# The last four expert turns: GpSimd drains, the last expert's second up product ahead of a down product, and its rows scaled by two engines

## The reference, cut to what matters

```
x = x + einsum(mix, w_out)
xf = rms_norm(x, g_ffn)
for each expert e, for the tokens that chose it:
    y = (silu(xf @ w1[e]) * (xf @ w3[e])) @ w2[e]      # 1024 -> 512 -> 1024
    x[token] += gate * y
```

## Time and profile before

| What | us |
|---|---|
| median of three runs | 1347.95 |
| the profiled execution | 1346.08 |
| its span, first to last instruction | 1344.3 |
| busy: PE, DVE, ACT, POOL | 1231.8, 418.8, 335.1, 279.5 |
| mean granted TensorE clock, share of full speed | 0.976 |

### The profile page before, as it was taken

How to read it: one execution, slowest core, us unless ns; L and a number is a source line. 1 busy time by engine, 2 the same in 40 slices (tenths; PEclk the granted TensorE clock), 3 DMA queues, 4 the chain that set the end, 5 groups by cost and what they waited for, 6 DMA issues and landing times.

```text
span 1344.3 us, 31662 instructions
## 1 busy us (share of the span) xinstructions
PE 1231.8 (92%) x13258; PEld 870.7 (65%) x13258; DVE 418.8 (31%) x906; ACT 335.1 (25%) x782; POOL 279.5 (21%) x401
## 2 busy tenths in 40 slices
PE   4999999998899999999999889987799899999983
PEld 2554444446556666666666588654689798888871
DVE  2431411116644555544543741111011111111110
ACT  3431020025435545535544100111000000000000
POOL 1320000103222312212111012322132223333211
PEclk9999999999999999999999889998999999999998
DMA  8611120133102201201033989999999999999993
GB/s 327 248 58 39 65 70 33 46 118 113 68 23 70 80 17 65 80 17 58 29 106 142 378 304 364 363 353 385 382 375 381 379 368 376 379 377 381 378 409 88
DMA packets 44844, 278.64 MB, mean 207 GB/s; under 512 B 10232, under 2 KB 15352, under 8 KB 31948
## 3 DMA queue, kind: packets, MB, share of 16 engines
q1 hardware_dynamic: 36656, 254.80, 49.3%
q0 software_dynamic: 6800, 17.84, 5.7%
q10 hardware_dynamic: 1296, 4.72, 1.0%
HBM read 250.49 MB, written 29.83 MB: 209 GB/s over the span
## 4 chain that ended last, share of the span: by engine, by line
PE 73%; DMA 12%; issue 6%; DVE 2%; ACT 2%; POOL 2%; SPq 1%; another core or an unknown queue 1%; ACTq 0%; POOLq 0%; DVEq 0%
PE psum L1093 17%; PE psum L1157 13%; DMA arena<-in_w 11%; PE psum L996 8%; PE psum L1214 7%; PE psum L1039 5%; PE psum L1071 3%; PE psum L1165 3%; PE psum L1051 2%; PE psum L869 2%; PE psum L940 2%; PE psum L1202 2%; PE psum L884 2%; PE psum L1148 1%; PE psum L1224 1%
## 5 line engine op out<-in xcount | busy, mean ns | idle before, releaser
L1157 PE MATMUL psum<-arena 128*64 128x80 f32 (+1 forms) x5632 | 229.9, 240 | 22.7 <-issue 13.2
L1093 PE MATMUL psum<-arena 128*128 128x512 f32 (+1 forms) x576 | 241.2, 577 | 1.4 <-DMA arena<-in_w_in 1.4
L1157 PEld LDWEIGHTS psum<-arena 128*64 128x64 f32 x5632 | 217.3, 138 | 34.8 <-issue 24.2
L1093 PEld LDWEIGHTS psum<-arena 128*128 128x128 f32 x576 | 109.1, 192 | 125.1 <-issue 124.6
L996 PE MATMUL psum<-arena 128*128 128x512 f32 x288 | 126.9, 593 | 1.8 <-DVE arena L2065 1.0
L1214 PE MATMUL psum<-arena 128*64 128x96 f32 (+1 forms) x2816 | 118.8, 244 | 9.5 <-issue 7.9
L1214 PEld LDWEIGHTS psum<-arena 128*64 128x64 f32 x2816 | 114.0, 139 | 13.4 <-issue 11.5
L1735 POOL DMA_INDIRECT out_y<-arena,index_now x54 | 75.3, 1395 | 194.4 <-ACT arena L1559 129.3
L1616 POOL TENSOR_SCALAR small<-small 128x2 f32<-128x2 f32 (+4 forms) x44 | 10.4, 236 | 453.3 <-DVE small L1813 163.6
L996 PEld LDWEIGHTS psum<-arena 128*128 128x128 f32 x288 | 53.3, 190 | 63.2 <-issue 61.5
L1559 ACT ACTIVATE arena<-psum,slot_gate 96x1024 f32<-96x1024 f32 x22 | 24.4, 1111 | 270.9 <-PE psum L1224 270.9
(11 more groups left out here) (251 smaller groups left out, 1367.1 us busy)
## 6 DMA issues: line engine op xcount, KB each, us to landing
arena<-in_w SPq DMA_DIRECT2D x96, 2048.0 KB, 24.0
z_rows<-arena SPq DMA_DIRECT2D x27, 256.0 KB, 2.0
arena<-z_rows SPq DMA_DIRECT2D x9, 768.0 KB, 5.6
arena<-in_w_in SPq DMA_DIRECT2D x3, 2048.0 KB, 21.6
arena<-in_x_rows ACTq DMA_DIRECT2D x9, 512.0 KB, 4.4
arena<-in_xT_rows SPq DMA_DIRECT2D x9, 512.0 KB, 13.3
arena<-in_x_rows SPq DMA_DIRECT2D x9, 512.0 KB, 6.3
out_y<-arena SPq DMA_DIRECT2D x9, 512.0 KB, 2.6
```

Of the source, the lines that this page charges most:

```text
L1093: ins = pe.matmul(o[:, 0:w], xT[n][:, k, :], w_in[:, at_ + k * w:at_ + (k + 1) * w], start=(k == 0), stop=(k == KD - 1))
L1157: ins = pe.matmul(o[c:c + CT, j * EB:j * EB + rows], w[:, k, j * P + c:j * P + c + CT], x[:, k, 0:rows], start=(k == 0), stop=(k == KD - 1))
```

## The change

It has three parts.

1. GpSimd. `turn(p)` begins with `pool.drain()` in its last four turns, 28 to 31.
2. The order at the last expert. SP issues the w3 of turn 31 ahead of the w2 of turn 30. PE does `hidden_3(31)` ahead of `down_by_tokens(30)`. The down product of turn 31 goes to PSUM bank 5 in place of bank 4, and doesn't wait for the reading of bank 4 any more.
3. The scaling of turn 31. ScalarE scales the lower 512 columns and VectorE the upper 512, from bank 5. VectorE raises a new semaphore `y_half`, and the last scatter waits for it beside `y_read`.

```diff
@@ SP
-                def between():
+                def down_before():
                     if p > FIRST:
                         load_down(sp_, p - 1, SETS[p - 1], before_it(p - 1) + 1)
-                load_ups(sp_, p, SETS[p], before_it(p) + 1, between)
+                load_ups(sp_, p, SETS[p], before_it(p) + 1, down_before if p < NE - 1 else lambda: None)
+                if p == NE - 1:
+                    down_before()
@@ PE, expert(p)
+                    if p == NE - 1:
+                        hidden_3(SETS[p], s, b, w3_in[SETS[p]], loads_of(p), rows)
                     downs_read(b - 2, p - 2)
                     down_by_tokens(SETS[q], q, w2_in[SETS[q]], loads_of(q))
...
-                hidden_3(SETS[p], s, b, w3_in[SETS[p]], loads_of(p) + more, rows)
+                if p < NE - 1:
+                    hidden_3(SETS[p], s, b, w3_in[SETS[p]], loads_of(p) + more, rows)
@@ PE, after turn 31
             hidden_back(last)
-            downs_read(last - 1, last - 1)
-            down_by_tokens(SETS[last], last, w2_in[SETS[last]], loads_of(last))
+            down_by_tokens(SETS[last], last, w2_in[SETS[last]], loads_of(last), 5)
@@ ACT, y_take_by_tokens, half=True in turn 31
+                if half:
+                    act.activation(ye[s][0:ET, 0:BANK], bank(5)[0:ET], ACT.Copy, scale=gate_col(col)[0:ET]).then_inc(y_read, 1)
+                    return
@@ POOL, scatter, finish=True in turn 31
                 pool.wait_ge(y_read, b + 1)
+                if finish:
+                    pool.wait_ge(y_half, 1)
                 pool.wait_ge(before, count)
@@ POOL, turn(p)
+                if p + 4 >= NE:
+                    pool.drain()
@@ DVE, after hT_take(31)
+            last = dve.value_load(order_e[0:1, NE - 1:NE], min_val=0, max_val=NE - 1)
+            dve.wait_ge(yT_full, NE)
+            dve.wait_ge(ye_out[1], stores_of(NE - 3))
+            TS(ye[1][0:ET, BANK:], bank(5)[CT:CT + ET], gate_hi[CT:CT + ET, bass.ds(last, 1)], None,
+               ALU.mult).then_inc(y_half, 1)
```

More of the change, by code:

```diff
@@ L537, in build @@
         hi_ok = sem("upper_slots_ready")
+        y_half = sem("last_y_upper_half")
         tab_ok, gather_idx, scatter_idx = sem("slot_tables_ready"), sem("gather_indices"), sem("scatter_indices")
@@ L1193, in hidden_back, with down_by_tokens @@
                 ins.then_inc(ht_full, 1)
-            def down_by_tokens(w, b, arrived, count):
+            def down_by_tokens(w, b, arrived, count, to=4):
                 pe.wait_ge(arrived, count)
@@ L1201, in down_by_tokens @@
                     for i, c in enumerate((0, CT)):
-                        ins = pe.matmul(bank(4)[c:c + CT], hT[:, at_:at_ + ET], w2s[w][:, k, i * BANK:(i + 1) * BANK],
+                        ins = pe.matmul(bank(to)[c:c + CT], hT[:, at_:at_ + ET], w2s[w][:, k, i * BANK:(i + 1) * BANK],
                                         start=(k == 0), stop=(k == KF - 1))
@@ L1559, in y_take, with y_take_by_tokens @@
                 act.activation(ye[s][0:EB], bank(6, 2)[0:EB], ACT.Copy, scale=gate_col(col)[0:EB]).then_inc(y_read, 1)
-            def y_take_by_tokens(s, b, col, out_sem, count):
+            def y_take_by_tokens(s, b, col, out_sem, count, half=False):
                 act.wait_ge(yT_full, b + 1)
                 act.wait_ge(out_sem, count)
+                if half:
+                    act.activation(ye[s][0:ET, 0:BANK], bank(5)[0:ET], ACT.Copy, scale=gate_col(col)[0:ET]).then_inc(y_read, 1)
+                    return
                 act.activation(ye[s][0:ET, 0:BANK], bank(4)[0:ET], ACT.Copy, scale=gate_col(col)[0:ET])
@@ L1578, in turn @@
                 if by_tokens(p):
-                    y_take_by_tokens(p % 2, b, e, ye_out[p % 2], count)
+                    y_take_by_tokens(p % 2, b, e, ye_out[p % 2], count, p == NE - 1)
                 else:
@@ L1736, in store, with scatter @@
                                         bounds_check=last_token, compute_op=ALU.add, oob_is_err=False).then_inc(signal, 16)
-            def scatter(s, b, e, signal, before, count, rows, parts):
+            def scatter(s, b, e, signal, before, count, rows, parts, finish=False):
                 if before is signal:
@@ L1764, in turn @@
                 before = (stores_of(p - 1) if p else 0) + more
-                scatter(s, b, e, ye_out[s], ye_out[1 - s], before, CAPS[p], out_parts(p))
+                scatter(s, b, e, ye_out[s], ye_out[1 - s], before, CAPS[p], out_parts(p), p == NE - 1)
             for s in range(2):
```

## The result

The changed kernel takes 1338.96 us (median of five runs, 1337.65 to 1344.6), the kernel before 1347.95 beside it. The ratio is 0.994, 95% interval [0.9915, 0.9965]. It was timed twice more, each time beside new runs of before: 0.9943 [0.9923, 0.9963] and 0.9947 [0.9931, 0.9964]. The mean of the three is 0.9943: it gains 0.57%, some 7.6 us. The forecast was 7.35 us. The intervals are wide beside that: the first allows 4.7 to 11.5 us.

A forecast was written before the change was run, and what follows sets the result against it. It took GpSimd's 8.8 us closing drain, with nothing beside it, to set the end. Closing drain and barrier save 8.65 us, a later last scatter costs 1.3: 1347.95 - 7.35 = 1340.6 us, range 1336.5 to 1346.

The forecast's parts named there:

- The drain's list: GpSimd's closing drain: 82 ns per DMA issued since the drain before, so 8.8 us falls to 0.15; chance 0.60.
- The first rival: Every GpSimd drain costs 8.8 us once DMAs have been issued; slower, 1355 to 1358 us; chance 0.09.
- the second: Closing drain stays at 8.8 us, belonging to the program's end, and the others cost nothing: 1349.3 us; chance 0.09.
- the third: A drain behind a GpSimd DMA has a floor of 2 us beside its list: 1344.4 us; chance 0.10.
- It waits for the landing: Turn 31: the drain lasts until turn 30's scatter lands; last scatter issued at landing + 0.1 + 1.0 + 0.8 us.
- The fourth rival: The list is right, but a drain doesn't wait for the landing: gain 8.45 us, 1339.5 us; chance 0.12.
- Turn 28's drain: 101 DMAs take 8.3 us, to 1287.9, hidden with 3.3 us to spare before that turn's scatter.
- Part 2, the start of the last down product: Last expert's new order: last down product starts at 1323.85, not 1324.25; gain 0.4 us, bounds 0 and 0.6.
- the sum: Whole execution: span falls by 8.65 - 1.3 = 7.35 us, median to 1340.6 us.
- Parts 2 and 3 bring nothing: Last scatter awaits turn 30's landing at 1329.6, so even without drains its issue is 1330.4, against 1330.20.
- VectorE's half: Turn 31's scaling of 512 columns on VectorE: between 0.42 us and twice that, taken as 0.7.

The follow-up runs named there:

- experiment 11: The changed kernel run again unaltered, on one chip beside the version with 18 idle transposes: 1340.43 us, ratio 0.9947.
- drain16: Kernel before with a single GpSimd drain between turns 15 and 16, 54 DMAs behind it: run once, 1345.93 us.
- experiment 10: Kernel before's order with halves, drains in turns 28 to 30 and 18 idle transposes ahead of turn 31's second up product: 1335.36 us, ratio 0.9902.
- experiment 6: Kernel before's order with the halves on ScalarE and VectorE (both from bank 4) and drains in turns 28 to 30 only: 1338.43 us, ratio 0.9946.
- experiment 1: Kernel before with the four drains alone: 1338.53 us, ratio 0.9953.
- experiment 2: Changed kernel without its drains, so new order and halves alone: 1349.36 us, ratio 1.0021.
- experiment 9: Changed kernel with eight idle transposes ahead of turn 30's down product and without turn 31's drain: 1336.87 us, ratio 0.9923.
- experiment 12: Repeat of kernel before's order with halves, drains in turns 28 to 30 and 18 idle transposes: 1335.91 us, ratio 0.9917.

## Why the prediction was right, and where its steps were not

**The drain's list: right.** A drain goes through the DMAs that GpSimd issued since the drain before. Five points, from closing drains that all began 0.4 to 0.5 us after the last landing: 107 DMAs 8.815 us, 54 DMAs 4.473, 6 DMAs 0.554, 2 DMAs 0.223, 1 DMA 0.129. From 6 to 54 that is (4.473 - 0.554)/48 = 81.6 ns each, from 54 to 107 (8.815 - 4.473)/53 = 81.9, with 0.05 left over. The prediction had 82 and a closing drain of 0.15. The first rival (a fixed cost), the second (the cost belongs to the end) and the third (a floor of 2 us) each fall by the row of 4473 or of 129 ns. The Trainium skill ("VectorE: DVE Perf Modes", "The DRAIN you can't avoid") has some 12 ns for the drains of start and end on all five engines. For GpSimd's closing drain that doesn't hold here: the shortest took 129 ns.

**It waits for the landing: right.** The drain of turn 31 ended 0.09 us after turn 30's landing in the changed kernel (1335.71 against 1335.62), and in the four other profiles that have it. The fourth rival falls. From that landing to the issue it was 1337.44 - 1335.62 = 1.82 us (forecast 1.9), from the last landing to the end 0.8 (forecast 0.85). Taking the drain away brought that to 0.91 and 0.93.

**Turn 28's drain: mis-sized.** Forecast 8.3 us from the end of the last issue; its row has 14.2, but it begins 2.7 us before that end (1280.22 against 1282.87), so 11.5 is the figure to compare. It held a wait that the 8.3 left out: the scatters of turn 27 landed at 1290.24, 7.4 after that end, and the drain ended 4.2 later still. The text had allowed for "some 7 us" more, a wait with the whole list behind it, and a scatter of turn 28 that slips without harm. It was 3.2 more, since half of the list was left behind the landing and not all of it (last section). And the scatter did not even slip: ScalarE still released it, with a wait of 2.04 us.

```profile
1281.55 1.32 POOL L1743 DMA_INDIRECT out_y<-arena,index_now  x1 [0.30 <-issue]
1295.16 0.18 POOL L1752 COPY index_now<-slot_hi 32x1 uint32 x1 [12.29 <-issue]
...
1297.50 1.43 POOL L1743 DMA_INDIRECT out_y<-arena,index_now  x1 [2.04 <-ACT arena L1564]
```

The spare time between the copy's end (1295.46) and the release was some 1.2 us and not 3.3. In all the other kernels that have it this drain took 14.2 to 14.5 us.

**Part 2, the start of the last down product: the step that failed.** "The down product of turn 30 (3.65) runs 1318.95 to 1322.6" held for the place and not for the length. Behind the new wait it takes 5.2 to 5.35 us in four of five unfilled profiles of the new order. I had priced a moved wait by when the product begins, and not by the clock at which it runs after it. In place of a gain of 0.4 the last down product starts 1.4 to 1.7 us after W; in the profile of before it was 0.5. This carries on to turn 30's scatter, issued 1330.83 - 1323.29 = 7.5 us after the product's start (forecast 6.0), and since the last scatter waits for that one's landing, to the end. The changed kernel's third profile (experiment 11) shows that nothing else in the step failed: there the clock stayed up, the last down product starts 0.05 us after W, a gain of 0.4, and turn 30's scatter is issued 6.0 us behind the product's start.

**Why the sum was right all the same.** Partly by luck. The forecast had the end at 1336.95 - 1323.78 = 13.2 us after W, and the changed kernel ended at 14.9, 14.9 and 13.6. But before's profile, from which the 7.35 us are counted, ended 1.6 to 1.8 us sooner than before seems to do as a rule. The old order has a wait in the same stretch, ahead of the up product. In the profile of before it was 2.15 us and the clock stayed up; in the three other unfilled profiles of that order it was 3.6 to 3.7, and the product took 5.2 to 6.2. The difference arose 20 us earlier, where the clock was low in before, in the down product of turn 29:

```profile
1297.02 6.29 PE L1214 MATMUL psum<-arena 128*64 128x80 f32 x128 [2.40 <-issue]
...
1297.50:1300.00 2.50, 2.50 (x43) 2.50 (x41) 0.00 (x0) 0.00 (x0) 0.00 (x0) 0.50 0.97 318
```

In the three others it took 4.65 us. So in before TensorE came some 1.5 us later to its last wait, and the wait was shorter by as much. The usual before pays the price of the clock in its last stretch too. Two profiles tell what it is there, each with its closing drain put back to 8.815: the drain16 kernel ends at 17.8 + 4.34 = W + 22.1, the drains alone at 13.6 + 8.69 = W + 22.3. Against the changed kernel's 14.9 that is 7.2 to 7.4 us, near the 7.6 of the timings. Few profiles stand behind this, and the agreement is closer than they warrant: by the same count the drains alone gain 8.7 us, and their timing says 6.3 (3.5 to 9.2). In parts, from 22.1 to 14.9: the closing drain -8.69, turn 31's drain +0.9, and the rest, +0.6, is order and halves.

**Parts 2 and 3 bring nothing: right, and for the reason given.** Without drains the issue stood 8.5 us after W, against 8.0 in drain16: 0.5 later (forecast 0.2). The halves wait for the landing in every profile of the new order. In the old order it is the other way round: turn 30's scatter is out earlier, and the halves are what counts (experiment 10, released by VectorE). From the start of the last down product to the last scatter's issue it is 5.48 us with them (experiment 6) and 5.95 without (experiment 1). The timing of experiment 2 says 0.21% slower, 2.8 us, of which the tail shows 0.4. Where the rest lies I can't tell; the interval begins at 0.06%, which is 0.8 us.

**VectorE's half**: 0.76 us, taken as 0.7.

## What to carry to other kernels

A drain of GpSimd at the end of a program pays for every DMA that GpSimd issued since its last drain, about 82 ns each in this kernel, on the path that sets the end. Drain once in a gap shortly before the end: one drain in turn 28 gave as much as four. Then let no drain stand between two scatters that already wait for each other. When an instruction is moved behind a longer wait of TensorE, price it at the lower clock too, and look at several executions of the kernel before, since one profile may have the clock low at another place than the next. Moving work earlier pays nothing if its consumer still waits for a landing; moving what that landing depends on does.

## What the hardware showed that I had not expected

**The clock after a wait is not decided by the wait's length alone.** Behind idle waits of TensorE of 2.50 to 3.68 us in this stretch the product took 5.2 to 6.2 us in eight of nine profiles; in the ninth, the changed kernel's third, it took 3.65 behind 2.65 us. Of the shorter ones, 2.15 us (before) kept the clock at 1.00, 1.91 (experiment 9) lost it, 1.61 and 1.56 kept it. The windows over wait and product of the changed kernel's third profile:

```profile
1315.80:1318.40 2.60, 0.00 (x0) 1.00 0.50 175
1318.50:1320.00 1.50, 1.50 (x8) 1.00 0.26 109
```

The down product of turn 29 says the same. Behind a wait of 2.1 us it kept the clock in the changed kernel's first and third profiles and lost it in experiments 2 and 12. Here are the changed kernel's first and experiment 12's:

```profile
1301.16 4.65 PE L1217 MATMUL psum<-arena 128*64 128x80 f32 x128 [2.10 <-issue]
...
1295.35 6.29 PE L1215 MATMUL psum<-arena 128*64 128x80 f32 x128 [2.10 <-issue]
```

What tips it is open.

Whether work in the wait keeps the clock up rests on one profile above all, experiment 10's: 3.7 us lay between the two products, 2.18 of them filled, and the clock stayed, where the four profiles of that order with as long a stretch and fewer transposes or none (8 in one) lost it. Experiment 12's is weaker: its stretch was 2.2 us, and before kept the clock over 2.15 with nothing in it. With 8 transposes in the new order one profile of two kept the clock, without them one of five, which shows nothing. The times speak for the 18: 0.9902 and 0.9917 with them, 0.9946 [0.9928, 0.9965] without. Lost, the clock makes a product of 3.65 us 1.5 to 2.6 us longer.

**A drain that has to wait leaves 41 ns for each DMA of its list behind the last landing.** Turn 28's, with 101 DMAs in its list, ended 4.18 us after the last landing, in all eleven profiles that have it. The one between turns 15 and 16, with 53, ended 2.22 us after it (1075.18 to 1077.40). Those of turns 29 and 30, with 2, ended 0.13 after it, and those of turn 31, with 1, 0.09. That is 41 ns each with 0.05 left over, half of the 82 that a DMA costs a drain which begins when all has landed. How long the drain waited makes no difference: turn 29's waited over 7 us for its two. Nor does the kind of DMA: the two long lists have gathers and scatters, those of turns 29 to 31 scatters alone. So half of the work seems to be done before the landing and half behind it. What the two halves are the traces don't show.
